# One list of slots instead of two programs: joining the front and back halves of an encoder layer

## The reference, cut to what matters

```python
h = x + 0.5 * post1(SwiGLU_1(pre1(x)))          # rms_norm before and after
u = pre_mix(h); z = u @ w_in                    # 42 tiles of 128 columns: q, k, v, rwkv, gates
A = diff_attention(z_q, z_k, z_v, ...)          # prompt: block-causal; samples: 1024 cached rows + 16
B = rwkv7_branch(z_rw, ...)                     # vector state, chunks of 64 tokens
m = sigmoid(gA) * (A @ w_o_att) + sigmoid(gB) * (B @ w_o_rwkv)
h = h + post_mix(m @ w_out)
y = h + 0.5 * post2(SwiGLU_2(pre2(h)))          # D_MODEL 1024, D_FF 2816
```

## Time and profile before

| | us |
|---|---|
| median of 3 runs (lowest, highest) | 3678.39 (3676.76, 3696.72) |
| the profiled execution | 3680.85 |
| its span, first to last instruction | 3679.0 |
| TensorE busy | 3263.2 (89%) |
| VectorE busy | 1882.2 (51%) |
| ScalarE busy | 1508.3 (41%) |
| mean granted clock of TensorE | 0.936 |

### The profile page before, as it was taken

The page is one execution under the profiler, slowest core; times in us unless marked ns, Lnnn a source line. Parts: engine busy times, 40 slices in busy tenths (PEclk is TensorE's granted clock), DMA queues, the critical chain, the costliest instruction groups (busy, mean ns, idle before and its releaser), DMA issues. The chain is left out here.

```text
span 3679.0 us, 63427 instructions
## 1 busy us (share of the span) xinstructions
PE 3263.2 (89%) x26037; PEld 2992.7 (81%) x26037; DVE 1882.2 (51%) x3362; ACT 1508.3 (41%) x2629; POOL 211.2 (6%) x389
## 2 busy tenths in 40 slices
PE   2999999999899999998976659999888899987995
PEld 2999998898888888987864548989866878887995
DVE  3445657333665674346533574444665545456543
ACT  2334446333443573333353453333334444334432
POOL 0000111000010100001100110000110000010000
PEclk7999999999999999998986789999987999998997
DMA  4444466433554655335520643334652566463444
GB/s 151 126 140 146 148 200 204 122 86 93 168 159 135 190 176 131 85 87 179 155 88 28 209 134 90 97 95 122 188 156 62 155 209 214 142 186 109 127 125 173
DMA packets 732368, 514.37 MB, mean 140 GB/s; under 512 B 79812, under 2 KB 693936, under 8 KB 732080
## 3 DMA queue, kind: packets, MB, share of 16 engines
q1 hardware_dynamic: 702512, 409.04, 37.8%
q0 software_dynamic: 29568, 101.27, 7.9%
HBM read 432.54 MB, written 77.66 MB: 139 GB/s over the span
## 5 line engine op out<-in xcount | busy, mean ns | idle before, releaser
L581 DVE TENSOR_TENSOR fr_wlo<-fr_raw,fr_whi 128x512 fp32r<-128x512 f32 (+1 forms) x660 | 449.3, 681 | 897.3 <-ACT fr_whi L489 895.9
L489 ACT ACTIVATE fr_whi<-fr_raw 128x512 fp32r<-128x512 f32 (+1 forms) x660 | 409.0, 621 | 905.2 <-PE ps L718 848.2
L968 DVE TENSOR_TENSOR bk_wlo<-bk_raw,bk_whi 128x512 fp32r<-128x512 f32 x504 | 341.2, 678 | 665.1 <-ACT bk_whi L880 664.4
L880 ACT ACTIVATE bk_whi<-bk_raw 128x512 fp32r<-128x512 f32 x504 | 311.5, 619 | 672.6 <-PE ps L1121 607.6
L718 PE MATMUL ps<-fr_hidhi,fr_whi 128*128 128x384 f32 x1536 | 552.5, 360 | 0.0
L718 PE MATMUL ps<-fr_hidlo,fr_whi 128*128 128x384 f32 x1536 | 522.5, 340 | 0.0
L718 PE MATMUL ps<-fr_hidhi,fr_wlo 128*128 128x384 f32 x1536 | 522.5, 340 | 0.0
L1121 PE MATMUL ps<-bk_xahi,bk_whi 128*128 128x384 f32 x1248 | 447.6, 359 | 5.9 <-DVE bk_gate L992 5.1
L1121 PE MATMUL ps<-bk_xalo,bk_whi 128*128 128x384 f32 x1248 | 425.6, 341 | 0.0
L1121 PE MATMUL ps<-bk_xahi,bk_wlo 128*128 128x384 f32 x1248 | 425.4, 341 | 0.0
L718 PE MATMUL ps<-fr_xahi,fr_whi 128*128 128x384 f32 x1056 | 372.2, 352 | 12.7 <-DVE fr_xalo L650 12.6
(11 more groups left out here) (411 smaller groups left out, 4753.8 us busy)
## 6 DMA issues: line engine op xcount, KB each, us to landing
fr_raw<-in_ffn_w_in_dram SPq DMA_DIRECT2D x264, 256.0 KB, 2.9
bk_raw<-in_ffn_w_in_dram SPq DMA_DIRECT2D x264, 256.0 KB, 2.9
fr_raw<-in_w_in_dram SPq DMA_DIRECT2D x252, 256.0 KB, 2.9
fr_raw<-in_ffn_w_out_dram SPq DMA_DIRECT2D x120, 256.0 KB, 2.6
bk_raw<-in_ffn_w_out_dram SPq DMA_DIRECT2D x120, 256.0 KB, 2.6
zT_scratch<-fr_zo POOLq DMA_DIRECT2D x126, 192.0 KB, 2.6
bk_area<-in_cache_att_k_dram SPq DMA_DIRECT2D x32, 512.0 KB, 4.5
bk_area<-in_cache_att_v_dram SPq DMA_DIRECT2D x32, 512.0 KB, 4.2
```

What stands on the lines that cost most here:

```text
L489: act.activation(w["hi"][:, s % RING, 0:x.n], raw[:, s % RING, 0:x.n], ACT.Copy).then_inc(whi, 1)
L581: dve.tensor_tensor(w["lo"][:, s % RING, 0:x.n], raw[:, s % RING, 0:x.n], w["hi"][:, s % RING, 0:x.n].bitcast(F32), ALU.subtract).then_inc ...
L880: act.activation(w["hi"][:, s % RING, 0:x.n], raw[:, s % RING, 0:x.n], ACT.Copy).then_inc(whi, 1)
L968: dve.tensor_tensor(w["lo"][:, s % RING, 0:x.n], raw[:, s % RING, 0:x.n], w["hi"][:, s % RING, 0:x.n].bitcast(F32), ALU.subtract).then_inc ...
```

## The change

The two programs become one, `trunk`, with one list, `trunk_plan` (1,282 slots, the same 1,164 slabs; the second feed-forward's kinds are now "G", "U", "D"), one set of buffers and one chain of background work: recurrence and attention of pieces 0, 1 and 2 and then the samples, each beginning where the one before ends (slots 226, 381, 468, 623, 710, 901 and 972, end at 1057). The branch products of piece 0 stand where 22 empty slots were, behind the last "d" (slots 608 to 623), followed by 4 empty slots; then the last z (628 to 711) and at once the output product of piece 0 (712), whose operand waits meanwhile in free tiles of `hid` (`m_of`). `take(T)` splits the loaded outputs; for piece 0 that is at slot 570, beside the last down-projection. The recurrence's tiles come every 10 steps, its output and the attention's norm are shortened, and the samples' attention goes on with the prompt attention's semaphores from their last counts. The gates use the z buffer `zo`.

```diff
-def front_plan():
...
+MIX_GAP, TAIL_GAP, Z_GAP = 20, 22, 4
...
+def trunk_plan():
+
+    down = lambda kind, T, groups: chained(unit_slabs(kind, T, k, TAIL if k == DT - 1 else groups) for k in range(DT))
+    branches = lambda T: chained(unit_slabs(kind, T, u, [(0, KS)]) for u in range(DT) for kind in "ab")
+    slots = [None] * 32 + chained(up_units("gu", 0, UP_ORDER)) + down("d", 0, DOWN_ORDER)
     for T in range(THIRDS):
-        slots += chained(up_units(T + 1, UP_ORDER[:EARLY])) if T + 1 < THIRDS else [None] * FRONT_GAP
+        slots += chained(up_units("gu", T + 1, UP_ORDER[:EARLY])) if T + 1 < THIRDS else branches(0) + [None] * Z_GAP
         z = [unit_slabs("z", T, m, HALVES) for m in Z_ORDER]
         slots += side_by_side(z[:BANKS]) + chained(z[BANKS:])
         if T + 1 < THIRDS:
-            slots += chained(up_units(T + 1, UP_ORDER[EARLY:])) + down(T + 1)
-    return number(slots)
...
-def back_plan():
-
-    slots = [None] * 10
+            slots += chained(up_units("gu", T + 1, UP_ORDER[EARLY:])) + down("d", T + 1, DOWN_ORDER)
     for T in range(THIRDS):
-        slots += chained(unit_slabs(kind, T, u, [(0, KS)]) for u in range(DT) for kind in "ab")
-        slots += chained(unit_slabs("o", T, u, HALVES) for u in range(DT))
-        slots += [None] * BACK_GAP
-        up = up_units(T, range(FT))
-        slots += side_by_side(up[:BANKS]) + chained(up[BANKS:])
-        slots += chained(unit_slabs("d", T, k, TAIL if k == DT - 1 else GROUPS) for k in range(DT))
-    return number(slots + [None] * FRONT_GAP)
+        if T >= 1:
+            slots += branches(T)
+        slots += chained(unit_slabs("o", T, u, HALVES) for u in range(DT)) + [None] * MIX_GAP
+        up = up_units("GU", T, range(FT))
+        slots += side_by_side(up[:BANKS]) + chained(up[BANKS:]) + down("D", T, GROUPS)
+    return number(slots + [None] * TAIL_GAP)
...
+        def m_of(h, T, u):
+            if T >= 1:
+                return hid[h][:, u]
+            return hid[h][:, DT + u] if u < BACK - DT else hid["lo"][:, BACK + 2 * (u - BACK + DT) + (h == "lo")]
...
+        begins = [plan.slot_of["z", 0, Z_ORDER[0], 0] + 2 * ZRT + 6]
+        for T in range(THIRDS):
             begins += [begins[-1] + mixer_end(T), begins[-1] + mixer_end(T) + a_steps(T)]
...
+        takes = [first_down[2] + 10, first_last[0] + 10, max(first_last[1] + 10, begins[-1] + s_steps + 8)]
...
+            def load_branches(T):
+                pool.wait_ge(used, up_end(THIRDS - 1) if T == 0 else plan.end("U", T - 1, FT - 1))
+                r_done(pool, T)
+                a_done(pool, T)
+                if T == THIRDS - 1:
+                    s_pool_end(pool)
+                for i, src in enumerate(("attT", "rwT")):
+                    pool.dma_start(x_raw[:, KS * i:KS * i + KS], feature_tiles(t[src], *tokens(T))).then_inc(x_in[i], 16)
...
+                    if T == THIRDS - 1 and n == z_no(T, Z_ORDER[0]):
+                        dve.wait_ge(mhi, DT)
+                        dve.wait_ge(mlo, DT)
...
-LORA_STEPS, TILE_STEPS, TILE_EVERY = LOAD_STEPS + 5, 16, 12
+LORA_STEPS, TILE_STEPS, TILE_EVERY = LOAD_STEPS + 5, 16, 10
...
-OUT_STEPS = 4
+OUT_STEPS = 3
...
-    return mixer_steps(T)[1] + (32 if T == THIRDS - 1 else 24)
+    return mixer_steps(T)[1] + RT * OUT_STEPS + (16 if T == THIRDS - 1 else 8)
...
+NORM_STEPS = HEADS + 4
...
-        return LOAD_STEPS + TURN_STEPS + LOAD_STEPS + UNIT_STEPS * len(units_of(T)) + 5 + 10
+        return LOAD_STEPS + TURN_STEPS + LOAD_STEPS + UNIT_STEPS * len(units_of(T)) + 5 + NORM_STEPS
...
-        front(nc, t, S)
-        back(nc, t, S)
+        trunk(nc, t, S)
```

More of the change, by code:

```diff
@@ L331, in rest, with trunk @@
         yield
[L334 to L341 removed]
+def trunk(nc, t, S):
+    with stage(nc, "tr_") as (ctx, sb, sem):
         ps = S["ps"]
@@ new lines, in along @@
+        def along(prepare, post, take, mix, final, mixer):
+            out = [(preps[0], prepare(0)), (preps[1], prepare(1)), (posts[0], post(0)), (preps[2], prepare(2)),
+                   (posts[1], post(1)), (takes[0], take(0)), (posts[2], post(2))] + mixer
+            for T in range(THIRDS):
+                out.append((mixes[T], mix(T)))
+                if T + 1 < THIRDS:
+                    out.append((takes[T + 1], take(T + 1)))
+                out.append((finals[T], final(T)))
+            return out
@@ L451, in body @@
             def body(i, x):
+                after = plan.slots[i + 1] if i + 1 < len(plan.slots) else None
+                if after is not None and after.kind == "a":
+                    load_gates(after.third, after.tile)
                 for T in range(THIRDS):
@@ L689, in _, with final @@
+            def final(T):
+                yield from scale_out("D", T)
+                for k in range(DT):
+                    residual("D", T, k, "ffn2_post_g")
+                    yield
             for s in range(AHEAD):
@@ L2084, in on_act @@
         width = prompt_of(T)
-        for step in range(10):
+        for step in range(NORM_STEPS):
             for h in range(HEADS):
```

806 lines of the change are left out of this document (296 added, 510 removed).

## The result

The changed kernel takes 3649.86 us, median of 4 runs (3645.58 to 3653.78), the kernel before 3684.14 in the same comparison: ratio 0.9906, 95% interval 0.989 to 0.9921. It is faster by 34 us, less than half of the 75.9 us forecast, and the time lies just above the range.

What follows compares the result with a forecast made beforehand. TensorE was busy 89% of the span, so slot cost and stretches without slots were taken to count. Taking away 178.5 us and giving back 102.6 gained 75.9: 3604.9 us profiled, 3602 median, range 3566 to 3645.

Steps and rivals of the forecast that it cites:

- Step 2: Before the merged stretch: eleven chunk slots move from the pause to beside dense work, 17.6 us more, bounds 10 and 22.
- Taken away (178.5): Removed: program change 80.1, last pause 42.2, old branch products 49.1, first output product's wait 7.1; together 178.5 us.
- Step 1: Merged stretch between last down-projection and last z product: VectorE has most work; 78 us plus 3 for attention's input, 81.
- Step 3: Last z product: more attention units lie before the Sigmoids, 282 us against 296.1, -14, bounds -35 and +10.
- Step 4: Pause behind the first piece's output product: two whole recurrence tiles fall into it, +10 us, bounds 0 and 15.
- Step 5: First piece's second feed-forward: up-projection -23 us, down-projection +22 as sample chunks slide into it, so 0, bounds -15 and +15.
- Step 6: Second piece's branch products: third recurrence's output steps now beside them, +12 us, bounds 0 and 20.
- Step 7: Second piece's pause holds fewer attention slots, -33 us; the background work given up lies beside the feed-forward, +25.
- Step 8: Handovers between recurrences and attentions have one step less: five at 0.8 us, +4, bounds 0 and 25.
- A: Rival that the filler does not fill: merged stretch at 95 us, 40 us less gain, 3642 us; chance 0.20.
- B: Rival that overlap is better than in any row: merged stretch at 66 us, whole 3573 us; chance 0.18.
- C: Slower rival: SP's queue becomes the bound, weight loads waiting at each of five handovers, 3705 us; chance 0.04.

Runs made afterwards that it cites:

- b_all3: Kernel before, two programs, with the changed kernel's three numbers (tiles every 10 steps, 3 output steps, 8 normalisation steps): 3688.77 us, ratio 1.0005.
- b_out3: Kernel before with 3 output steps instead of 4 and 8 normalisation steps instead of 10, tiles still every 12 steps: 3712.02 us, ratio 1.0074.
- b_tile10: Kernel before with the recurrence's tiles every 10 steps instead of 12 and nothing else: 3722.74 us, ratio 1.0112.
- a_lag4_second: Changed kernel with everything of the second attention four slots further behind its input loads: 3648.91 us, ratio 0.9893.
- a_gates_first: Changed kernel with the 16 gate tiles (those with a Sigmoid) put first in the last z product: 3646.74 us, ratio 0.9899.
- a_t12_third: Changed kernel with the recurrence's tiles every 12 steps in the third piece alone: 3648.07 us, ratio 0.991.
- a_unfilled: Changed kernel, one list, with the pause before the last z product empty again and the first piece's branch products behind that product: 3701.38 us, ratio 1.0045.
- a_tile12_first: Changed kernel with tiles every 12 steps in the first piece, and by a slip the second and third pieces' tile loads four slots sooner: 3688.91 us, ratio 1.0009.

## Why the prediction failed, step by step

**Step 2, chunks leave the pause (17.6 us, bounds 10 and 22), is the one that failed.** It was the only charge ahead of the merged stretch beside the handovers, and the stages up to there took 52.5 us more. What it priced came out as priced: from the first chunk on, 79 slots took 278.6 us where 61 took 219.9, 21.2 more than the 18 bare slots between them, inside its bounds. What it left out is that the tiles, packed from 12 to 10 steps and in the second piece begun 12 slots sooner, cost 6.5 us more in the first recurrence and 19.8 in the second. The step put that at nothing: it took the work of a tile as fixed, however close and wherever it stands. Between the two recurrences lie another 4.8, the first handover in them (11.7 us of wait against 4.6, 5.3 to 11.7 in equal kernels). 21.2 + 6.5 + 19.8 + 4.8 make the 52.5 but for rounding. That the new numbers, not the join, bring it is shown by b_all3; that spacing and place share the 26 about equally, by b_out3 and b_tile10. Which engine's order makes a place dear is open.

Of the 48.9 us by which the span's gain missed the forecast (27.0 against 75.9), 34.9 are here. Steps 4 and 7 add 13.0 and 9.8, and steps 6 and 1 take back 17.0 and 6.5.

**Taken away (178.5).** The 80.1, 42.2 and 49.1 us went. Of the 7.1 us at the output product 3.5 went (44.7 against 48.2).

**Step 1, the merged stretch (81, bounds 66 and 95):** 74.5, VectorE 0.80 busy (59.5 us), about as said. I had 3 us in it for the attention's input; the wait was 16.1, and a_lag4_second shows what the stretch takes without it, 58.6. The sum over VectorE's instructions was thus too high by about 20 us, 14 of them because part of its 108 instructions slid out of the stretch (98 are in it, 59.5 us and not 73.5), and the wait too low by 13. That the sum came near is luck: the two misses cancel. GpSimd issued its gate loads in 0.717 us there as well. What was drawn from the Trainium skill, "GPSIMD Engine Reference", section Specifications, on SBUF interfaces shared with VectorE, that the issues would be drawn out, is thus not borne out by this trace either; the section itself speaks of contention and not of issuing a transfer.

**Step 3, the last z product (-14):** -7.3. The mechanism, units beside Sigmoids, is shown by a_gates_first, and the size is off by 7. That the product would answer so steeply to four slots (+18.5) was not in the working.

**Step 4, the first pause (+10, bounds 0 and 15):** +23.0. With the old spacing (a_t12_third) it is +10.8, so 12.2 are the spacing: the same omission as in step 2. Why the other 10.8 come was not tested; the working put them down to the two whole tiles.

**Step 5 (0):** +5.2 (313.4 + 139.0 against 329.6 + 117.6), inside its bounds; the up-projection shrank by 16 and the down-projection grew by 21, where 23 and 22 were worked out.

**Step 6 (+12, bounds 0 and 20):** -5.0, the wrong sign: VectorE did more there (44.5 us instead of 38.9) in less time, at clock 1.00 instead of 0.87.

**Step 7 (-33 and +25):** -26.9 and +28.7.

**Step 8 (+4, bounds 0 and 25):** +7.1 at the first handover, a size at which equal kernels differ, and the second is the 16.1 us of step 1, where empty slots stood in place of z slabs: inside the bounds, above the value.

**The rivals.** The time came out near A (3642), by luck: A had the filled stretch at 95 and it was 74.5, and its name, the filler does not fill, is refuted by a_unfilled. B did not happen. C's mechanism, SyncE's queue, was not worse in the changed kernel: ScalarE waited 90.4 us in all for weights there, 120.6 before. With the tile loads four slots sooner in that queue (a_tile12_first) it was 158.9.

**The signs.** Most of those with a size came: the merged stretch in 70 to 90 us, the pause behind the second output product at 53.4, the down-projections of the second feed-forward 21.4 and 17.5 us longer, the z product at 288.8 for 280. None of them looked at the stages ahead of the merged stretch, where the error was.

## What to carry to other kernels

When a change tightens the schedule to make room for its main idea, price the tightening by itself: put its numbers into the old kernel. Background work is not a fixed sum that may be moved about; what stands beside it, above all functions with other tables on ScalarE, can raise a slot's price by half (4.9 us against 3.3 here). And an edit that moves the time by nothing may have bought something that a neighbour takes back: look at the stages, then fix the neighbour.

## What the runs showed of the hardware

- A table load on ScalarE took 1.283 us every time. Exp and Sigmoid in turn made 18 slots 88.6 us long that took 59.5 without, 29.2 us for 26.5 us of loads and Sigmoids, and the granted clock stood at 0.83 instead of 1.00.
- Ending one program and beginning the next on the same core cost 38.2 us in which TensorE was busy 1.6 us, when the program before had no work left over (b_all3). The first loads of the second program are in it, so it is no price of the change alone.
- The first use of an attention's five input loads came 11.9 us after the first was issued (1744.53 to 1756.39 us) with 2.7 MB in flight. With only four empty slots between, TensorE waited 16.1 us; with four slots of z besides (a_lag4_second) it had no wait for these loads.
